# Two transformer blocks on one core: the first feed-forward chunk as wide pairs, banks in two sets, row factors spread through DRAM

## The chip, the cores and the metric

One NeuronCore of a Trainium2 chip. The metric is the device time of one execution in microseconds, lower is better. All data are float32 in and out.

## The reference, cut to what matters

A first block (retention and differential attention), then a second block of two layers. 256 tokens, width 1024. The change touches the four feed-forward networks (FFNs) of the second block and the projections for keys and values (kv) and queries (q):

```python
def rms_norm_2(x, g):
    xf = x.astype(jnp.float32)
    y = xf * lax.rsqrt(jnp.mean(xf * xf, axis=-1, keepdims=True) + RMS_EPS)
    return (y * g.astype(jnp.float32)).astype(x.dtype)

def swiglu_ffn(x, w_gate, w_up, w_down):            # D = 1024, F = 2816
    return (jax.nn.silu(x @ w_gate) * (x @ w_up)) @ w_down
...
    for layer in range(DEPTH_2):                    # 2 layers
        h = h + HALF_STEP * swiglu_ffn(rms_norm_2(h, ffn1_norm[layer]), ...)
        u = rms_norm_2(h, mix_norm[layer])
        ...                                         # layer 0: convolution; layer 1: stick-breaking attention,
                                                    # q from u, k and v from one projection after layer 0
        h = h + HALF_STEP * swiglu_ffn(rms_norm_2(h, ffn2_norm[layer]), ...)
```

## The kernel before, in words

The program is written out by hand per engine, with semaphores; nothing schedules it. Each engine's instructions stand in the order of its code. The stages of the second block are ffn1a, pw1, pw2 (convolution), ffn2a, kv, ffn1b, q, stick attention, o, ffn2b.

**Weights** come in slabs of 4 x 128 rows by 512 columns. SP loads slab k into one of four slots of `raw`; ACT rounds it (`cast`, L1174, `whi`), DVE takes the rest (`low`, L1550, `wlo`), so that a product in full precision is made of three products: high by high, low by high, high by low. The activations stand turned in `aT`, high and low halves side by side (`aT_hi`, `aT_lo`, 256 tokens each). A slot of `whi` is free when PE has done with the slab that held it (`half_done`, two counts a slab).

**FFN up side.** 2816 hidden columns are 11 chunks of 256 gate and 256 up columns, each chunk two slabs (half 0 and half 1 of the 1024 rows). Weights are the stationary operand, so hidden units come out on partitions. There are two forms. `turned_slab` (L639): per tile and row block three matmuls of 256 columns (L654, L656, L658) into one half bank, 48 a slab. `wide_slab` (L663): per tile and row block a pair, `wlo` by `aT_hi` in 256 columns (L678) and `whi` by both halves of `aT` in 512 (L680), 16 pairs a slab; the left half of a bank then holds the main sum and the right half a low sum, which must be added: ACT copies it out (`low_products`, L1351), DVE adds (`summed`, L1855, L1860). Chunk 0 of each FFN is turned, chunks 1 to 10 are wide. Chunks take pairs of banks in a ring of three pairs (`ffn_pair`: two of `acc`, one `att`), two pairs a chunk. PSUM's fourth pair is `tp`, for transposes. The order of slabs is (0, half 0), (1, half 0), (0, half 1), (1, half 1), then plain.

The rms norm's gain goes into `aT`, but its row factor `rs` does not: it depends on statistics that come late. It is applied to gate sums, where tokens lie along the free axis, so the 256 factors must lie in a row in each partition (`rsb`). DVE makes two diagonals from `rs` (`diagonal`, L1822), PE multiplies them with a matrix of ones (`spread_rs`, L692, in fp32), DVE copies the result (`rs_rows`, L1828). That is done in ffn1a, ffn2a, kv, q and ffn2b; ffn1b uses the factors of kv, and has dummy products in that place (L746). The up sum needs no factor: `rs_down`, half of it, is applied with the down product.

**Leaving a stage.** The second half of `h` is summed only after the last down slab, so four of eight blocks of `aT` are made inside the next stage: PE turns them into `tp` (`exit_fills`, L701) behind the first slab, ACT writes the high part (L1187), DVE the low part (L1565), and PE waits for `tp_lo` before the third slab. POOL makes `rs` from the statistics (L481 and L485, `residual_rs`). In ffn2b bank pair `att` holds part of the attention's output until the sum of the stage before.

```python
            order = [(0, 0), (1, 0), (0, 1), (1, 1)]          # pair_order
            ring = [acc_pair[(g + 1) % 2], att_pair, acc_pair[g % 2]]
            return ring[(2 * (c - 1) + up) % 3]               # ffn_pair
```

## Time and profile before

| | us |
|---|---|
| median of 3 runs (1265.23 to 1265.76) | 1265.34 |
| profiled execution | 1266.64 |
| its span, first to last instruction | 1264.9 |
| PE busy | 1255.5 (99%) |
| DVE busy | 827.1 (65%) |
| ACT busy | 619.9 (49%) |
| POOL busy | 85.1 (7%) |
| HBM read | 223 MB, 177 GB/s |
| mean granted clock of PE | 0.999 |

How to read it: a matmul's duration in the timeline runs from its start to its modelled end, and the next one starts before that, so what matmuls cost is read from starts. PE's share says that it is the engine to look at; what the others do shows only where PE waits for them.

### The profile page before, as it was taken

How to read it: one execution, taken by the hardware profiler on the slowest of the kernel's cores; microseconds unless marked ns; L12 is line 12 of the kernel's file. 1: busy time of each engine (PE TensorE's matmuls, PEld its weight loads, DVE VectorE, ACT ScalarE, POOL GpSimd, SP SyncE). 2: the span in 40 equal slices, each digit the busy share in tenths (PEclk: the TensorE clock that was granted, in tenths of full speed). 3: DMA queues.
4: the chain of work that ended last, by engine and by line, in shares of the span. 5: the costliest groups of instructions: out<-in, count | busy, mean ns of one | idle time of the engine just before them, and what ended most of it. 6: DMA issues, size and time to landing. Idle time of an engine off the chain costs nothing.

```text
span 1264.9 us, 16671 instructions
## 1 busy us (share of the span) xinstructions
PE 1255.5 (99%) x6814; PEld 1074.5 (85%) x6814; DVE 827.1 (65%) x953; ACT 619.9 (49%) x765; POOL 85.1 (7%) x122
## 2 busy tenths in 40 slices
PE   9999999999999999999999999999999999999998
PEld 7888877888988888879888889898888988988886
DVE  6565577667667656676777655656765666876653
ACT  5354566543555534444555543445553454555542
POOL 2223010101000002001000000000000110100000
PEclk9999999999999999999999999999999999999999
DMA  9654544456655566534565655656655513666640
GB/s 311 208 158 162 198 136 141 164 195 199 195 188 183 176 224 219 185 125 151 190 192 183 200 168 190 200 167 199 200 168 199 170 64 111 210 196 200 200 166 34
DMA packets 165388, 225.28 MB, mean 178 GB/s; under 512 B 7520, under 2 KB 106436, under 8 KB 165312
## 3 DMA queue, kind: packets, MB, share of 16 engines
q1 hardware_dynamic: 163488, 220.23, 53.3%
q0 software_dynamic: 1808, 3.98, 1.1%
q8 instruction: 54, 0.88, 0.3%
q14 instruction: 22, 0.18, 0.0%
q10 hardware_dynamic: 16, 0.00, 0.0%
HBM read 223.14 MB, written 1.05 MB: 177 GB/s over the span
## 4 chain that ended last, share of the span: by engine, by line
PE 97%; DVE 2%; ACT 1%; DMA 0%; issue 0%; SPq 0%; ACTq 0%
PE acc L680 15%; PE acc L621 15%; PE acc L623 15%; PE acc L622 15%; PE att L680 8%; PE acc L678 8%; PE att L678 4%; PE acc L654 2%; PE acc L658 2%; PE acc L656 2%; PE tp L701 1%; PE att L621 1%; PE att L623 1%; PE att L622 1%; DVE wlo L1550 1%; ACT whi L1174 0%
## 5 line engine op out<-in xcount | busy, mean ns | idle before, releaser
L1550 DVE TENSOR_TENSOR wlo<-raw,whi 128x2048 fp32r<-128x2048 f32 x205 | 467.7, 2289 | 165.4 <-ACT whi L1174 165.4
L1174 ACT ACTIVATE whi<-raw 128x2048 fp32r<-128x2048 f32 x205 | 388.6, 1912 | 92.8 <-PE acc L623 80.1
L680 PE MATMUL acc<-aT,whi 128*128 128x512 f32 x832 | 290.9, 391 | 0.0
L678 PE MATMUL acc<-aT,wlo 128*128 128x256 f32 x832 | 233.6, 281 | 0.0
L680 PEld LDWEIGHTS acc<-aT,whi 128*128 128x128 f32 x832 | 155.6, 187 | 33.8
L621 PE MATMUL acc<-whi,aT 128*128 128x512 f32 x432 | 172.9, 400 | 0.5 <-DVE wlo L1638 0.5
L623 PE MATMUL acc<-wlo,aT 128*128 128x512 f32 x432 | 168.9, 391 | 0.0
L622 PE MATMUL acc<-whi,aT 128*128 128x512 f32 x432 | 168.7, 391 | 0.0
L680 PE MATMUL att<-aT,whi 128*128 128x512 f32 x448 | 157.8, 391 | 0.0
L678 PEld LDWEIGHTS acc<-aT,wlo 128*128 128x128 f32 x832 | 157.3, 189 | 0.0
L621 PE MATMUL acc<-whi,hT_hi 128*128 128x512 f32 x348 | 135.7, 390 | 0.0
L622 PE MATMUL acc<-whi,hT_lo 128*128 128x512 f32 x348 | 135.5, 389 | 0.0
L623 PE MATMUL acc<-wlo,hT_hi 128*128 128x512 f32 x348 | 135.4, 389 | 0.0
L678 PE MATMUL att<-aT,wlo 128*128 128x256 f32 x448 | 125.4, 280 | 0.0
L680 PEld LDWEIGHTS att<-aT,whi 128*128 128x128 f32 x448 | 83.8, 187 | 18.4
L621 PEld LDWEIGHTS acc<-whi,aT 128*128 128x128 f32 x432 | 81.4, 188 | 18.2 <-issue 1.4
L623 PEld LDWEIGHTS acc<-wlo,aT 128*128 128x128 f32 x432 | 81.4, 188 | 17.6
L622 PEld LDWEIGHTS acc<-whi,aT 128*128 128x128 f32 x432 | 81.5, 189 | 15.9
L1351 ACT ACTIVATE low_part<-acc 128x512 f32<-128x512 f32 x52 | 31.0, 596 | 124.4 <-PE acc L680 124.4
L678 PEld LDWEIGHTS att<-aT,wlo 128*128 128x128 f32 x448 | 84.7, 189 | 0.0
L623 PEld LDWEIGHTS acc<-wlo,hT_hi 128*128 128x128 f32 x348 | 65.3, 188 | 13.6
L622 PEld LDWEIGHTS acc<-whi,hT_lo 128*128 128x128 f32 x348 | 65.3, 188 | 13.4
(332 smaller groups left out, 1588.1 us busy)
## 6 DMA issues: line engine op xcount, KB each, us to landing
raw<-in_ffn_w_gate_dram SPq DMA_DIRECT2D x88, 512.0 KB, 4.0
raw<-in_ffn_w_up_dram SPq DMA_DIRECT2D x88, 512.0 KB, 5.1
raw<-in_ffn_w_down_dram SPq DMA_DIRECT2D x88, 512.0 KB, 4.8
raw<-in_w_in_dram SPq DMA_DIRECT2D x70, 512.0 KB, 4.8
raw<-in_conv_w_pw_dram SPq DMA_DIRECT2D x24, 512.0 KB, 4.9
raw<-in_w_kv_dram SPq DMA_DIRECT2D x16, 512.0 KB, 5.0
raw<-in_ret_w_o_dram SPq DMA_DIRECT2D x8, 512.0 KB, 4.3
raw<-in_diff_w_o_dram SPq DMA_DIRECT2D x8, 512.0 KB, 4.2
```

Of the source, the lines that this page charges most:

```text
L621: mm_(banks[t][:, :], tokens(Th, kt, t), hi_, start=first_ and j == 0, stop=False)
L622: mm_(banks[t][:, :], tokens(Tl, kt, t), hi_, start=False, stop=False)
L623: last = mm_(banks[t][:, :], tokens(Th, kt, t), lo_, start=False, stop=last_ and j == len(kts) - 1)
L654: mm_(dst, whi[:, slot, cols], aT_hi[:, kt, :], start=half == 0 and j == 0 and n == 0, stop=False, skip_group_check=True)
L656: mm_(dst, whi[:, slot, cols], aT_lo[:, kt, :], start=False, stop=False, skip_group_check=True)
L658: last = mm_(dst, wlo[:, slot, cols], aT_hi[:, kt, :], start=False, stop=half == 1 and j == SLAB_K - 1, skip_group_check=True)
L678: mm_(bank[:, 0:T], wlo[:, slot, cols], aT_hi[:, kt, :], start=half == 0 and j == 0, stop=False, skip_group_check=True)
L680: last = mm_(bank[:, :], whi[:, slot, cols], aT[:, kt, :, :].rearrange("p a n -> p (a n)"), start=False, stop=half == 1 and j == SLAB_K - ...
L701: last = nc.tensor.transpose(tp[b % 2][:, q * T + t * P:q * T + (t + 1) * P], src(kt, t), ident[:, :])
L1174: A_(whi[:, slot, :], raw[:, slot, :], ACT.Copy).then_inc(hi_ready, 1)
L1351: A_(low_part[:, up, :, :], ffn_pair(name, c, up)[:, :, T:CW], ACT.Copy)\
L1550: V.tensor_tensor(wlo[:, slot, :], raw[:, slot, :], whi[:, slot, :].bitcast(F32), ALU.subtract)\
```

## The change

Chunk 0 of each FFN is made of wide pairs too. The chunks alternate between two sets of two pairs: even chunks take one `acc` pair and `att`, odd ones the other `acc` pair and `tp` (in ffn2b chunk 0 takes both `acc` pairs, chunk 1 `att` and `tp`). Since chunk 1's up part now lies in `tp`, where the fills of `aT` are still being read, PE's order is: chunk 0 half 0; the fills; chunk 1 half 0 gate part only; chunk 0 half 1; chunk 1 half 0 up part; chunk 1 half 1. The row factors are no longer spread by PE: POOL writes `rs` to a row in DRAM with two DMAs, waits, and reads it back into all partitions with one. The diagonals, the products and the copies go.

```diff
@@ build
         def ffn_pair(name, c, up):
 
             g = PLACE[name].g
-            ring = [acc_pair[(g + 1) % 2], att_pair, acc_pair[g % 2]]
-            return ring[(2 * (c - 1) + up) % 3]
+            first, second = acc_pair[g % 2], acc_pair[(g + 1) % 2]
+            if name == "ffn2b" and c < 2:
+                return [[first, second], [att_pair, tp_pair]][c][up]
+            return [[first, att_pair], [second, tp_pair]][c % 2][up]
 
 
         GAIN_STEP = 8
...
@@ build, engine POOL
                 pool.wait_ge(stat_ready, use + 1)
                 rsqrt(rs[:, use, :], rs_tmp[:, use, :], rs_tmp[:, use, :], 1.0, EPS, rs_ready)
                 pool.wait_ge(rs_ready, use + 1)
+                if use in SPREAD_USES:
+                    n = SPREAD_USES.index(use)
+                    for t in range(TT):
+                        pool.dma_start(rs_row[n, t * P:(t + 1) * P].rearrange("(p a) -> p a", a=1),
+                                       rs[:, use, t:t + 1]).then_inc(rs_written, 16)
                 nc.gpsimd.tensor_scalar(rs_down[:, use, :], rs[:, use, :], 0.5, None, ALU.mult)\
                     .then_inc(rs_down_ready, 1)
+                if use in SPREAD_USES:
+                    pool.wait_ge(rs_written, 32 * (n + 1))
+                    pool.dma_start(rsb[:, :], rs_row[n:n + 1, :].to_broadcast([P, T])).then_inc(rsb_ready, 16)
 
             residual_rs(RS_X)
             pool.wait_ge(rs_ready, 1)
...
@@ build, engine PE
                     if n == 1:
                         last.then_inc(half_done, 1)
 
-            def wide_slab(k, name, c, half):
+            def wide_slab(k, name, c, half, sides=(0, 1)):
 
                 w = PLACE[name]
                 pe.wait_ge(lo_ready, k + 1)
                 slot = k % SLOTS
-                for up in range(2):
+                for up in sides:
                     if half == 0 and c >= 2:
-
-                        pe.wait_ge(acc_free, 2 * (w.g + c - 1) + (up - 1) + 1)
+                        other = name == "ffn2b" and (c, up) == (2, 1)
+                        pe.wait_ge(acc_free, 2 * (w.g + c - 2) + up + 1 + other)
                     for n in range(FW // P):
                         bank = ffn_pair(name, c, up)[:, n, :]
                         f = up * (FW // P) + n
...
                                        stop=half == 1 and j == SLAB_K - 1, skip_group_check=True)
                     last.then_inc(half_done, 1)
 
-            def spread_rs(name, bank):
-
-                n = SPREADS.index(name)
-                pe.wait_ge(rdiag_ready, n + 1)
-                if n == 0:
-                    pe.wait_ge(pool_ready, 3)
-                for t in range(TT):
-                    last = mm_(bank[:, t * P:(t + 1) * P], ones[:, :], rdiag[:, t, :], start=True, stop=True)
-                last.then_inc(rsb_mm, 1)
-
             def fill(b, src, kts):
 
                 if b >= 2:
...
 
             def ffn_pe(name):
                 w = PLACE[name]
+                pe.wait_ge(tp_lo, w.b - 2)
+                pe.wait_ge(acc_free, 2 * (w.g - 1))
+                wide_slab(w.k, name, 0, 0)
                 if name == "ffn1b":
-                    pe.wait_ge(rsb_ready, SPREADS.index("kv") + 1)
-                for s, (c, half) in enumerate(pair_order(FC)):
-                    if s == 1 and name == "ffn1b":
-                        pe.wait_ge(acc_free, 2 * (w.g - 1) + 2)
-                        pe.wait_ge(rows_kept, 4)
-                        mm_(tp[0][:, 0:P], ones[:, :], ones[:, :], start=True, stop=True)
-                    elif s == 1:
-                        exit_fills(w.b - 2, w.g - 1, 1)
-                    pe.wait_ge(tp_lo, w.b - 2 if s < 2 else w.b)
-                    if c == 0:
-                        turned_slab(w.k + s, w.g, half)
-                    else:
-                        wide_slab(w.k + s, name, c, half)
-                    if s == 2 and name in SPREADS:
-                        spread_rs(name, tp[0])
-                    elif s == 2:
-                        for _ in range(TT):
-                            mm_(tp[0][:, 0:P], ones[:, :], ones[:, :], start=True, stop=True)
+                    pe.wait_ge(acc_free, 2 * (w.g - 1) + 2)
+                    pe.wait_ge(rows_kept, 4)
+                    pe.wait_ge(pool_ready, 3)
+                    mm_(tp[0][:, 0:P], ones[:, :], ones[:, :], start=True, stop=True)
+                else:
+                    exit_fills(w.b - 2, w.g - 1, 1)
+                wide_slab(w.k + 1, name, 1, 0, (0,))
+                pe.wait_ge(tp_lo, w.b)
+                wide_slab(w.k + 2, name, 0, 1)
+                wide_slab(w.k + 1, name, 1, 0, (1,))
+                wide_slab(w.k + 3, name, 1, 1)
+                for c in range(2, FC):
+                    for half in range(2):
+                        wide_slab(w.k + 2 * c + half, name, c, half)
                 ready = FC * FFN_AT[name]
                 for s in range(DOWN_SLABS):
                     k = w.k + 2 * FC + s
...
-                            pe.wait_ge(acc_free, 2 * (g - 1) + 1)
+                            pe.wait_ge(acc_free, 2 * (g - 2) + 1)
...
-                        if name in SPREADS:
-                            pe.wait_ge(rsb_ready, SPREADS.index(name) + 1)
                         exit_fills(w.b, w.g + FC, 0)
 
...
@@ build, engine ACT
 
                 def low_products(c):
                     for up in range(2):
-                        done(w.k + 2 * c + 1, up)
+                        if c:
+                            done(w.k + 2 * c + 1, up)
+                        else:
+                            act.wait_ge(half_done, 2 * w.k + 4 + up)
                         act.wait_ge(acc_free, 2 * (w.g + c))
                         A_(low_part[:, up, :, :], ffn_pair(name, c, up)[:, :, T:CW], ACT.Copy)\
                             .then_inc(low_copied, 1)
...
                     exit_hi(w.b - 2, 1, gain_in)
                 cast(w.k + 1 + AHEAD)
                 cast(w.k + 2 + AHEAD)
+                low_products(0)
                 silu(0)
-                cast(w.k + 3 + AHEAD)
+                cast(w.k + 3 + AHEAD, late=2)
                 for s in range(4, 2 * FC):
                     if s % 2 == 0:
                         low_products(s // 2 - 1)
...
@@ build, engine DVE
                                                       ALU.mult, ALU.mult)
                     last.then_inc(od_ready, 1)
 
-            def diagonal(use):
-
-                dve.wait_ge(rs_ready, use + 1)
-                for t in range(TT):
-                    last = V.tensor_scalar(rdiag[:, t, :], ident[:, :], rs[:, use, t:t + 1], None, ALU.mult)
-                last.then_inc(rdiag_ready, 1)
-
-            def rs_rows(name, bank):
-                n = SPREADS.index(name) + 1
-                dve.wait_ge(rsb_mm, n)
-                V.tensor_copy(rsb[:, :], bank[:, 0:T]).then_inc(rsb_ready, 1)
-                dve.wait_ge(rsb_ready, n)
+            def rs_rows(name):
+
+                dve.wait_ge(rsb_ready, 16 * (SPREADS.index(name) + 1))
 
             def turned_out(dst, g, ready, scale):
 
...
                     k = w.k + 2 * c + 1 if c else w.k + 2
                     gate, up = act_out[:, c % 2, :, :], hid[:, c % 2, :, :]
                     dve.wait_ge(lo_ready, k + AHEAD + 1)
-                    if c:
-                        dve.wait_ge(low_copied, copied + 2 * c - 1)
-                        V.tensor_tensor(gate, ffn_pair(name, c, 0)[:, :, 0:T], low_part[:, 0, :, :], ALU.add)\
-                            .then_inc(acc_free, 1)
-                        dve.wait_ge(acc_free, 2 * (w.g + c) + 1)
-                        V.tensor_tensor(gate, gate, spread, ALU.mult).then_inc(gate_ready, 1)
-                        dve.wait_ge(low_copied, copied + 2 * c)
-                        V.tensor_tensor(up, ffn_pair(name, c, 1)[:, :, 0:T], low_part[:, 1, :, :], ALU.add)\
-                            .then_inc(acc_free, 1)
-                    else:
-                        done(k, 1)
-                        one = [acc[w.g % 2][bank].rearrange("p (f n) -> p f n", n=T) for bank in range(2)]
-                        V.tensor_tensor(gate, one[0], spread, ALU.mult).then_inc(gate_ready, 1)
-                        dve.wait_ge(gate_ready, before + 1)
-                        V.tensor_copy(up, one[1]).then_inc(acc_free, 2)
+                    dve.wait_ge(low_copied, copied + 2 * c + 1)
+                    V.tensor_tensor(gate, ffn_pair(name, c, 0)[:, :, 0:T], low_part[:, 0, :, :], ALU.add)\
+                        .then_inc(acc_free, 1)
+                    dve.wait_ge(acc_free, 2 * (w.g + c) + 1)
+                    V.tensor_tensor(gate, gate, spread, ALU.mult).then_inc(gate_ready, 1)
+                    dve.wait_ge(low_copied, copied + 2 * c + 2)
+                    V.tensor_tensor(up, ffn_pair(name, c, 1)[:, :, 0:T], low_part[:, 1, :, :], ALU.add)\
+                        .then_inc(acc_free, 1)
 
                 def multiplied(c):
                     dve.wait_ge(silu_made, before + c + 1)
...
                 else:
                     exit_lo(w.b - 2, 1, gain_in)
                 low(w.k + 1 + AHEAD)
-                if name in SPREADS:
-                    diagonal(use)
                 low(w.k + 2 + AHEAD)
                 if name in SPREADS:
-                    rs_rows(name, tp[0])
+                    rs_rows(name)
                 summed(0)
                 low(w.k + 3 + AHEAD)
                 multiplied(0)
...
                     leave_ffn("ffn1b", RS_MIXB)
                 if s == 1:
                     exit_lo(pq.b - 2, 1, "mixb")
-                if s == 2:
-                    diagonal(RS_MIXB)
                 if s == 3:
-                    rs_rows("q", att[0])
+                    rs_rows("q")
 
                     turned_out(qT[:, 0:4, :], pq.g, lambda bank: dve.wait_ge(half_done, 2 * pq.k + 4 + bank),
                                SDK ** -0.5)
```

How it moves instructions, at three places.

PE in ffn2b, at the wait for `aT` (`tp_lo`) before chunk 0's second half. Before:

```order
L680 MATMUL att<-aT,whi 128x512
L678 MATMUL att<-aT,wlo 128x256
L680 MATMUL att<-aT,whi 128x512
L654 MATMUL acc<-aT,whi 128x256 [waits lo_ready,tp_lo]
L656 MATMUL acc<-aT,whi 128x256
```

After:

```order
L691 MATMUL att<-aT,whi 128x512
L689 MATMUL att<-aT,wlo 128x256
L691 MATMUL att<-aT,whi 128x512
L689 MATMUL acc<-aT,wlo 128x256 [waits lo_ready,tp_lo]
L691 MATMUL acc<-aT,whi 128x512
```

Before, `att` is chunk 1's up part, and 16 pairs stand between the fills and this wait; after, it is the gate part, and 8 do.

ACT in ffn2b, behind the casts of the slabs that chunks 0 and 1 need. Before:

```order
L1174 ACTIVATE whi<-raw 128x2048 [waits half_done,slab_landed3]
L1356 ACT_TABLE_LOAD
L1356 ACTIVATE act_out<-act_out 128x512 [waits gate_scaled]
L1174 ACTIVATE whi<-raw 128x2048 [waits half_done,slab_landed0]
L1351 ACTIVATE low_part<-acc 128x512 [waits acc_free,half_done]
L1351 ACTIVATE low_part<-att 128x512 [waits acc_free,half_done]
```

After:

```order
L1169 ACTIVATE whi<-raw 128x2048 [waits half_done,slab_landed3]
L1349 ACTIVATE low_part<-acc 128x512 [waits acc_free,half_done] x2
L1354 ACT_TABLE_LOAD
L1354 ACTIVATE act_out<-act_out 128x512 [waits gate_scaled]
L1169 ACTIVATE whi<-raw 128x2048 [waits half_done,slab_landed0]
L1349 ACTIVATE low_part<-att 128x512 [waits acc_free,half_done]
L1349 ACTIVATE low_part<-tp 128x512 [waits acc_free,half_done]
```

Two copies of chunk 0 stand ahead of the first silu; the next cast stands behind the silu in both.

POOL at the start of q. Before:

```order
L481 TENSOR_SCALAR rs_tmp<-rs_tmp 128x2 [waits stat_ready]
L485 TENSOR_TENSOR rs<-rs_tmp,mhalf 128x2 [waits pool_step]
L492 TENSOR_SCALAR rs_down<-rs 128x2 [waits rs_ready]
L581 MEMSET ntri 128x128 [waits half_done]
L582 AFFINE_SELECT ntri<-ntri 128x128 [waits pool_step]
```

After:

```order
L484 TENSOR_SCALAR rs_tmp<-rs_tmp 128x2 [waits stat_ready]
L488 TENSOR_TENSOR rs<-rs_tmp,mhalf 128x2 [waits pool_step]
L498 DMA rms_rows<-rs 128x1 [waits rs_ready]
L498 DMA rms_rows<-rs 128x1
L500 TENSOR_SCALAR rs_down<-rs 128x2
L504 DMA rsb<-rms_rows 128x256 [waits rms_row_written]
L592 MEMSET ntri 128x128 [waits half_done]
L593 AFFINE_SELECT ntri<-ntri 128x128 [waits pool_step]
```

Two DMAs, a wait for both to land and a third DMA stand between `rs` and the masks of the stick attention.

## Rows read from the trace of the kernel before

**Rows 1.** The page's busy shares, then the line of its chain by engine.
```profile
PE 1255.5 (99%) x6814; PEld 1074.5 (85%) x6814; DVE 827.1 (65%) x953; ACT 619.9 (49%) x765; POOL 85.1 (7%) x122
...
PE 97%; DVE 2%; ACT 1%; DMA 0%; issue 0%; SPq 0%; ACTq 0%
```

**Rows 2.** Waits of PE over the whole span: us in total, times, longest; first and last of five.
```profile
PE att L785 <- POOL ident L471: 1.6, 1, 1.6
...
PE att L621 <- DVE aT L2001: 0.2, 1, 0.2
```

**Rows 3.** Timeline of PE, ffn1a: start us, us, engine, line, operation.
```profile
310.77 0.28 PE L654 MATMUL acc<-aT,whi 128*128 128x256 f32 x1
...
316.52 1.03 PE L701 MATMUL tp<-ident,h 128*128 128x128 f32 x8
317.31 0.36 PE L678 MATMUL acc<-aT,wlo 128*128 128x256 f32 x1
```

**Rows 4.** Timeline of PE, ffn1a, from the spreading products to the down products.
```profile
328.69 0.61 PE L692 MATMUL tp<-rdiag,ones 128*128 128x128 f32 x4
329.05 0.36 PE L678 MATMUL acc<-aT,wlo 128*128 128x256 f32 x1
...
434.53 0.40 PE L621 MATMUL acc<-whi,hT_hi 128*128 128x512 f32 x1
```

**Rows 5.** Groups of PE by form: count | busy us, mean ns | idle before.
```profile
L746 PE MATMUL tp<-ones 128*128 128x128 f32 x4 | 0.6, 274 | 0.0
```

**Rows 6.** Timeline of DVE, ffn1a.
```profile
318.03 1.66 DVE L1565 SCALAR_TENSOR_TENSOR aT<-tp,gain,aT 128x256 fp32r<-128x256 f32 x4 [1.72 <-ACT aT L1187]
...
329.33 0.42 DVE L1828 COPY rsb<-tp 128x256 f32<-128x256 f32 x1 [3.88 <-PE tp L692]
```

**Rows 7.** Timeline, start of ffn2b: DVE, PE, ACT and DVE.
```profile
1083.14 1.65 DVE L1565 SCALAR_TENSOR_TENSOR aT<-tp,gain,aT 128x256 fp32r<-128x256 f32 x4
...
1074.95 0.28 PE L654 MATMUL acc<-aT,whi 128*128 128x256 f32 x1
...
1094.70 0.63 ACT L1356 ACTIVATE act_out<-act_out 128x512 f32<-128x512 f32 x1 [6.88 <-DVE act_out L1865]
...
1099.98 0.68 DVE L1855 TENSOR_TENSOR act_out<-acc,low_part 128x512 f32<-128x512 f32 x1
```

**Rows 8.** Timeline of POOL: a DMA issue, and rs of ffn2b.
```profile
32.10 0.57 POOL L504 DMA_DIRECT2D v_r<-in_diff_lq_dram  x1
...
1083.35 0.70 POOL L485 TENSOR_TENSOR rs<-rs_tmp,mhalf 128x2 f32<-128x2 f32 x1
```

**Rows 9.** DMA issues of POOL and one of SP: KB each, median us from issue to landing.
```profile
h<-in_x_dram POOLq DMA_DIRECT2D x2, 512.0 KB, 4.3
...
out_dram<-h SPq DMA_DIRECT2D x2, 512.0 KB, 2.8
...
g_out<-in_final_norm_dram POOLq DMA_DIRECT2D x1, 512.0 KB, 6.6
...
v_r<-in_diff_lk_dram POOLq DMA_DIRECT2D x2, 32.0 KB, 7.0
...
dqk_g<-in_diff_q_norm_g_dram POOLq DMA_DIRECT2D x2, 0.2 KB, 4.3
```

**Rows 10.** Timeline of PE and POOL, stage q.
```profile
1016.63 0.70 PE L1090 MATMUL att<-qT,kT 64*128 64x256 f32 x4
...
1002.70 0.70 POOL L485 TENSOR_TENSOR rs<-rs_tmp,mhalf 128x2 f32<-128x2 f32 x1
```

**Rows 11.** Timeline of PE and POOL, start of ffn2a.
```profile
583.42 0.28 PE L654 MATMUL acc<-aT,whi 128*128 128x256 f32 x1
...
588.16 2.62 POOL L485 TENSOR_TENSOR rs<-rs_tmp,mhalf 128x2 f32<-128x2 f32 x1
```

**Rows 12.** Instructions of line 481: ns min/median/max; and DVE's timeline beside issues.
```profile
L481 POOL TENSOR_SCALAR rs_tmp<-rs_tmp x7: 183/2164/2171, 24.1 to 1081.1; 128x2 f32<-128x2 f32 x7
...
30.34 2.29 DVE L1550 TENSOR_TENSOR wlo<-raw,whi 128x2048 fp32r<-128x2048 f32 x1
```

More of the change, by code:

```diff
@@ L218, in build @@
         ones = sb("ones", [P, P], to=second)
-        rdiag = sb("rdiag", [P, TT, P], to=second)
         rsb = sb("rsb", [P, T], to=second)
@@ L1068, in _ @@
                     slab(pkv.k + s, pkv.g + c, half, aT_hi, aT_lo)
-                if s == 2:
-                    spread_rs("kv", att[0])
             ffn_pe("ffn1b")
@@ L1078, in _ @@
             turned_slab(pq.k + 2, pq.g, 1)
-            spread_rs("q", att[0])
             turned_slab(pq.k + 1, pq.g + 1, 0, range(2, 4))
@@ L2061, in _ @@
                     kept_lo(pkv.b, 0, "ffn1b")
-                if s == 2:
-                    diagonal(RS_KV)
                 if s == 3:
-                    rs_rows("kv", att[0])
+                    rs_rows("kv")
                 if s in (3, 4):
```

7 lines of the change are left out of this document (4 added, 3 removed).

## The prediction

> **What bounds the kernel now.** I read the page's busy shares and its chain first, then PE's waits, then the timeline at the places that the change touches. PE is busy for 1255.5 of 1264.9 us, and 97% of the chain that ended last is PE [rows 1]. PE's list of waits has five entries, from 1.6 us down to 0.2, none in an FFN, in kv or in q [rows 2]. So time is won or lost in two ways only: fewer or cheaper PE instructions, and new waits of PE. DVE (65%) and ACT (49%) matter only where PE would wait for them. The clock granted to PE is 9 tenths or more in all slices of the page and 0.999 in the mean, its level of 2.4 GHz, with PE busy throughout.
>
> The profiled execution took 1266.64 us, 1.30 above the median of the three timed runs (1265.34). I make the sum against the profiled one and take the same off the median. A measurement of this kernel can tell about 0.2%, 2.5 us, from no change.
>
> **Cheaper products of chunk 0.** A turned slab is 48 matmuls of 256 columns. The first of ffn1a runs from 310.77 to the transposes at 316.52: 5.75 us [rows 3]. A wide slab is 16 pairs. From 329.05 to the first down product at 434.53 stand 19 slabs, 304 pairs, in 105.48 us: 0.347 us a pair, 5.55 a slab [rows 4]. Each of four FFNs has two turned slabs: 8 x 0.20 = **1.6 us** less of PE, all on the path.
>
> **Spreading products gone.** The diagonal matmuls of ffn1a take PE from 328.69 to 329.05, and the first matmul behind them lasts 0.36 us where one behind other such products lasts 0.28: 0.44 us [rows 3, 4]. By the code there are five such places (ffn1a, ffn2a, kv, q, ffn2b), and the dummies of L746 in ffn1b are four matmuls of the same form [rows 5]. 6 x 0.44 = **2.6 us**, all on the path. PE has 4.2 us less in all.
>
> **What is added beside PE, at nothing.** Per FFN: two ACT copies of low products (0.6 us each, as the page's L1351) and one DVE operation of 0.7 more; DVE loses two diagonals and a copy. In ffn1a DVE stood idle for 3.88 us before its copy of the row factors [rows 6], and ACT waited for DVE meanwhile. If that cover went, the delay would lie in the path costed below. Chunks from 2 up now wait for the chunk two before instead of the one before, so their slack grows. The factors, though, come by a slower way.
>
> **The split of chunk 1.** PE waits for the last two fills of aT before chunk 0's second half. Before, 16 pairs covered the copies; now 8 do (2.78 us, and 0.08 for the change from transposes). In ffn1a DVE begins them at 318.03 and needs 1.66, so ends 3.17 after the transposes began; these take 0.79, so PE now comes 0.79 + 2.86 = 3.65 after their start: 0.4 in hand [rows 3, 6]. In ffn2b DVE does a low part first and ends the copies at 1083.14 + 1.65 = 1084.79. There PE starts at 1074.95, and comes at 1074.95 + 5.55 + 0.79 + 2.86 = 1084.15 [rows 7]. **A new wait of 0.7 us**, with 0.06 for the semaphore. Everything behind it in PE's queue moves by as much.
>
> **The factors through DRAM.** This cost is in no row, and it decides the result. POOL writes rs in two DMAs of 4-byte pieces, waits for both, and issues a DMA that lands 128 copies of one 1 KB row. From the end of rs it takes 0.1 us to the first issue, 0.57 to the second [rows 8], then a landing, 0.1, then a landing. Call the sum c. The nearest row for the write is dqk_g, 4-byte pieces over partitions, 4.3 us: I take 4.5. For the read there are 4.3 (x again) and 6.6 (g_out, a broadcast), of 512 KB each [rows 9]; I take 5.1, the lower half, as it has a quarter of their bytes. **c = 10.3 us**. Bounds: 2.8 twice (the output's stores, another queue, nothing beside them) gives 6.4; 7.0 twice (v_r) gives 14.8.
>
> Where does PE feel c? In **ffn2b** chunk 2's up part goes into att, which chunk 1's gate must have left. When the factors land, DVE adds and scales gate 0 (two operations of 0.7, 1.4); then silu, the cast, the low part, the multiply and the add of gate 1 follow, in the rows of before from 1094.70 to 1099.98 + 0.68: 5.96 [rows 7]. With latencies 7.45 us. PE gets there, behind the wait above, at 1084.85 + 5.55 + 2.78 + 5.55 + 2.78 = 1101.51. So the factors must land by 1094.06. Rs is ready at 1083.35 + 0.70 = 1084.05 [rows 8]. Limit: c = 10.0. With 10.3, **0.3 us of wait**. In **q**, PE reaches the first stick score at 1016.63 - 0.44 = 1016.2 and needs both qT scalings (1.3 us) done. Rs ends at 1002.70 + 0.70 = 1003.40: limit c = 11.4 [rows 10]; no wait. Kv needs the factors a slab of 5.75 later than q, so c = 17 would do there. In the ring of ffn2a the rs ends 590.78 - 583.42 = 7.4 us into the stage, and the wait is for chunk 0 or for the low part of slab 5, at most 7.45 us behind the factors; PE comes 5 x 5.55 + 0.87 = 28.6 us into the stage, so c = 13.7 is free [rows 11]; ffn1a has an earlier rs. POOL now blocks until the write has landed. Behind it stand the masks of the stick attention and the final gain, with 5 us and more to spare.
>
> **Sum.** 4.2 - 0.7 - 0.3 = 3.2 us less: 1266.64 goes to 1263.4, the median 1265.34 to **1262.1**.
>
> One thing could stretch c. POOL's arithmetic is held while DVE runs L1550: L481 has a median of 2.16 us beside it and a minimum of 0.18. Its DMA issues aren't: L504 takes 0.57 at 32.10, beside the L1550 from 30.34 to 32.63 [rows 8, 12]. The Trainium skill, "SBUF — State Buffer", section "Who interferes with whom", says that a DVE operation with two SBUF inputs contends with GpSimd's reads, and infers that descriptor writing needs the write side. The trace agrees. The same page's box on DVE blocking DMA says that descriptor writing starves under the two-port modes; stretched to L1550 that rule would be the rival "held issues" below.
>
> **Rivals.**
> *Short way* (chance 0.25). c is under 10 and the 0.3 goes: 1265.34 - 4.2 + 0.7 = 1261.8. For it: the output's stores landed in 2.8 us. Against: 0.2 KB took 4.3 on this queue [rows 9]. The Trainium skill, "DMA: Bandwidth & Descriptors", section "Anatomy of one DMA — SWDGE (gpsimd) path", gives some 2 us plus the bytes for one such DMA: an estimate of c near 5 by that page, which is this case. No row here is as short.
> *Forecast* (0.35): c from 10 to 11, 1261.8 to 1262.8.
> *Longer way* (0.20). Above 11.4 q pays too: the waits are 0.7 + (c - 10.0) + (c - 11.4). c = 12 gives 1264.4, c = 13 gives 1266.4.
> *Held issues* (0.07). The second write of ffn2b, issued at 1084.7, is held by an L1550 for 2.3 us, q's read by some 1.4: waits of 2.6 and 0.3 beside the 0.7, 1264.7. Against it stands the 0.57 above.
> *Slower* (0.13): the round trip becomes the bound. From c = 13.7 the waits (0.7 + 3.7 + 2.3 = 6.7) pass the 4.2 by 0.2%; at 14.8 they are 0.7 + 4.8 + 3.4, with 1.1 in ffn2a's ring: 1271.1. For it: v_r landed in 7.0 us, and a write of 4-byte pieces to DRAM is in no row. Against: v_r stood in a filled queue, these don't.
> That the change doesn't do what it says gets no chance: which instructions go is plain from the order.
>
> **The numbers.** Faster by over 0.2% means under 1262.8: short way and forecast, 0.60. Within: longer way and held issues, 0.27. Slower: 0.13. The range goes from 1261.0 (no wait at all gives 1261.1) to 1267.0, which leaves out the slower case and little else.
>
> **What would show it.** PE: no threes of 256-column matmuls in the FFNs, no diagonals, pairs at 0.347 in chunk 0 too. A wait of PE for aT in ffn2b of 0.7, none in ffn1a. From the end of rs to the landing of rsb 10.3 us, in five places. A wait of PE at chunk 2's up part in ffn2b of 0.3, none before the stick scores. I am wrong if c is above 11.4, if PE waits in ffn1a, ffn2a or kv, or if the pairs of chunk 0 are slower.

## The result, and the profile after

The changed kernel takes 1291.09 us (median of 4 runs, 1288.58 to 1294.64), the kernel before 1265.43 (4 runs, 1265.23 to 1265.76): ratio 1.0202, 95% interval 1.0190 to 1.0214. It is **2.0% slower**; the forecast was 1262.1, with 1261.0 to 1267.0 as its range. The profiled execution took 1290.27 us, with a span of 1288.5 and a mean granted clock of 0.991.

The page's busy shares and the chain by engine, against [rows 1]:

```profile
PE 1261.3 (98%) x6662; PEld 1071.5 (83%) x6662; DVE 825.1 (64%) x942; ACT 624.1 (48%) x773; POOL 97.3 (8%) x137
...
PE 88%; DMA 5%; DVE 3%; POOL 1%; ACT 1%; issue 1%; SPq 0%; ACTq 0%; DVEq 0%
```

PE has 152 instructions fewer and is busy for 5.8 us *more*, and DMA now holds 5% of the chain, where it had none. The waits of PE, against [rows 2] (engine, line waited for: us in total, times, longest):

```profile
PE acc L689 <- DVE act_out L1844: 8.7, 3, 4.3
PE att L1085 <- DVE qT L1825: 6.9, 1, 6.9
PE att L783 <- POOL ident L474: 1.6, 1, 1.6
PE acc L632 <- issue: 1.4, 1, 1.4
PE att L689 <- DVE act_out L1844: 1.2, 1, 1.2
...
PE acc L689 <- DVE aT L1564: 0.4, 1, 0.4
```

All but the third are new, 18.6 us in sum. And what DVE waited for in front of them:

```profile
DVE act_out L1844 <- DMA rsb<-rms_rows: 34.5, 3, 13.5
DVE qT L1825 <- DMA rsb<-rms_rows: 9.6, 1, 9.6
DVE kT L1825 <- DMA rsb<-rms_rows: 8.2, 1, 8.2
```

So the row factors come late in all five places. Timeline of POOL and DVE in ffn2b, against [rows 7, 8]:

```profile
1098.65 0.72 POOL L488 TENSOR_TENSOR rs<-rs_tmp,mhalf 128x2 f32<-128x2 f32 x1
1099.66 1.18 POOL L498 DMA_DIRECT2D rms_rows<-rs  x2 [0.30 <-POOL rs L488]
1100.87 3.70 POOL L500 TENSOR_SCALAR rs_down<-rs 128x2 f32<-128x2 f32 x1
1110.98 0.59 POOL L504 DMA_DIRECT2D rsb<-rms_rows  x1 [6.42 <-DMA rms_rows<-rs]
1118.00 0.69 DVE L1844 TENSOR_TENSOR act_out<-acc,low_part 128x512 f32<-128x512 f32 x1 [13.51 <-DMA rsb<-rms_rows]
```

Rs ends at 1099.37, the writes are issued from 1099.66, the read only 11.3 us later, and DVE starts on the factors at 1118.00: c, the way from the end of rs to the landed factors, is 18.6 us. Counted alike, c is 17.9 in ffn1a, 17.7 in ffn2a, 18.6 in kv, 18.4 in q; the forecast had 10.3. The page's two entries for the new DMAs (KB each, median us to landing), against [rows 9]:

```profile
rsb<-rms_rows POOLq DMA_DIRECT2D x5, 128.0 KB, 7.0
...
rms_rows<-rs POOLq DMA_DIRECT2D x10, 0.5 KB, 9.4
```

The second cost is what the waits do to PE's clock. Windows of the trace (us; busy time and count of PE, PEld, DVE, ACT, POOL; granted clock; DMA share; GB/s) behind the four longest waits, in ffn1a, ffn2a, q and ffn2b:

```profile
334.00:340.00 6.00, 4.74 (x18) 4.15 (x19) 3.65 (x4) 3.40 (x4) 0.00 (x0) 0.72 0.13 44
612.00:617.00 5.00, 5.00 (x22) 4.30 (x21) 3.10 (x4) 3.40 (x4) 0.00 (x0) 0.66 0.00 0
1028.00:1034.00 6.00, 4.68 (x26) 3.94 (x27) 3.41 (x5) 1.96 (x3) 0.00 (x0) 0.50 0.06 19
1119.00:1124.00 5.00, 5.00 (x16) 4.11 (x16) 3.10 (x3) 3.40 (x4) 0.00 (x0) 0.50 0.02 6
```

A granted 0.50 is the level of 1.2 GHz. Behind each of these waits PE's products run at that level for 3.4 to 5 us: a pair starts every 0.64 us, not every 0.347. The waits before them were 1.8, 2.5, 6.9 and 4.3 us. In kv, where PE is held for 1.4 us, the clock doesn't fall.

Stage by stage, by the same operation in both timelines: ffn1a +2.9 us, ffn2a +3.5, kv +1.1, ffn1b -0.8, q to the first stick score +6.5, from there to the first cumulative product +2.7 (8.0 us for 5.3), ffn2b with the stick stage's rest +8.6. That is 24.5. The profiled execution was 0.6 ahead of that of before when ffn1a began (the transposes of ffn1a's entry start at 303.78 and were at 304.41), so it is 23.9 behind at ffn2b's down products; the spans differ by 23.6.

### The profile page after: what moved, and what is told of

Read it like the earlier page. It is cut to its first block, busy times and chain, and to the rows that moved or that the text cites. A ratio compares the mean times of both kernels' runs of the same rounds, so it can differ in the third digit from the quotient of the medians.

```text
span 1288.5 us, 16337 instructions
## 1 busy us (share of the span) xinstructions
PE 1261.3 (98%) x6662; PEld 1071.5 (83%) x6662; DVE 825.1 (64%) x942; ACT 624.1 (48%) x773; POOL 97.3 (8%) x137
## 4 chain that ended last, share of the span: by engine, by line
PE 88%; DMA 5%; DVE 3%; POOL 1%; ACT 1%; issue 1%; SPq 0%; ACTq 0%; DVEq 0%
PE acc L632 14%; PE acc L634 14%; PE acc L633 14%; PE acc L691 11%; PE att L691 6%; PE acc L689 6%; PE tp L691 5%; PE att L689 3%; DMA rms_rows<-rs 3%; PE tp L689 3%; DMA rsb<-rms_rows 2%; PE tp L702 1%; DVE wlo L1549 1%; PE acc L665 1%; PE acc L667 1%
## 5 line engine op out<-in xcount | busy, mean ns | idle before, releaser
L1549 DVE TENSOR_TENSOR wlo<-raw,whi 128x2048 fp32r<-128x2048 f32 x205 | 467.2, 2289 | 166.2 <-ACT whi L1169 166.1
L691 PE MATMUL acc<-aT,whi 128*128 128x512 f32 x704 | 253.4, 398 | 0.0
L689 PE MATMUL acc<-aT,wlo 128*128 128x256 f32 x704 | 200.4, 285 | 9.1 <-DVE act_out L1844 8.7
L691 PEld LDWEIGHTS acc<-aT,whi 128*128 128x128 f32 x704 | 134.5, 191 | 29.8
L689 PEld LDWEIGHTS acc<-aT,wlo 128*128 128x128 f32 x704 | 135.6, 193 | 10.4 <-issue 9.5
L691 PE MATMUL att<-aT,whi 128*128 128x512 f32 x384 | 135.4, 392 | 0.0
L691 PE MATMUL tp<-aT,whi 128*128 128x512 f32 x320 | 112.8, 391 | 0.0
L689 PE MATMUL att<-aT,wlo 128*128 128x256 f32 x384 | 107.7, 281 | 1.2 <-DVE act_out L1844 1.2
L689 PE MATMUL tp<-aT,wlo 128*128 128x256 f32 x320 | 89.6, 280 | 0.0
L691 PEld LDWEIGHTS att<-aT,whi 128*128 128x128 f32 x384 | 71.8, 187 | 15.9
L1349 ACT ACTIVATE low_part<-acc 128x512 f32<-128x512 f32 x44 | 26.2, 595 | 113.2 <-PE acc L691 113.2
```

Source lines behind the costliest of these rows:

```text
L689: mm_(bank[:, 0:T], wlo[:, slot, cols], aT_hi[:, kt, :], start=half == 0 and j == 0, stop=False, skip_group_check=True)
L691: last = mm_(bank[:, :], whi[:, slot, cols], aT[:, kt, :, :].rearrange("p a n -> p (a n)"), start=False, stop=half == 1 and j == SLAB_K - ...
L1349: A_(low_part[:, up, :, :], ffn_pair(name, c, up)[:, :, T:CW], ACT.Copy)\
L1549: V.tensor_tensor(wlo[:, slot, :], raw[:, slot, :], whi[:, slot, :].bitcast(F32), ALU.subtract)\
```

## Experiments

**1 and 2. Each half of the change alone.** The first kernel keeps the wide pairs, the two sets of banks and the split of chunk 1, and has TensorE spread the factors as before. The second is the kernel before with the factors sent through DRAM.

```diff
 # wide_pe_spread, on the changed kernel
-                        pool.dma_start(rs_row[n, t * P:(t + 1) * P].rearrange("(p a) -> p a", a=1),
-                                       rs[:, use, t:t + 1]).then_inc(rs_written, 16)
...
-                    pool.dma_start(rsb[:, :], rs_row[n:n + 1, :].to_broadcast([P, T])).then_inc(rsb_ready, 16)
...
-                wide_slab(w.k + 2, name, 0, 1)
+                if name in SPREADS:
+                    wide_slab(w.k + 2, name, 0, 1, (0,))
+                    spread_rs(name, tp[0])
+                    wide_slab(w.k + 2, name, 0, 1, (1,))
```

> The change with PE's own spreading put back (diagonal products into tp between the two sides of chunk 0's second half), wide pairs and bank sets kept. Theory A (the slow way of the factors makes all of the loss, the wide pairs are a gain): 8 x 0.20 and 0.44 for the dummies less, some 0.5 for the wait for aT in ffn2b, so 1263.9 (1263 to 1265.5), no wait of PE at chunk 2 and a granted clock of 0.999. Theory B (the new banks or the split order lose too): 1268 or more, with waits of PE in the first slabs of the FFNs.

> The kernel before with only the spreading changed: the factors go through DRAM, chunk 0 stays turned, the ring of three pairs stays. Theory A: some 18 us from rs to the landed factors in five places; since in the old ring chunk 2's up part waits for chunk 1's gate in every FFN, the delays are larger than in the change: about 5.7, 6.5 and 9 us in ffn1a, ffn2a and ffn2b, 1.5 in kv, 7 in q with 2.7 behind it at the lower clock, less 2.2 of products: 1290 to 1297. Theory B: under 1280.

The wide pairs alone: **1264.38 us** (10 runs), ratio to before 0.9992 (0.9983 to 1.0001), and PE's only new entry in the list of waits is 0.4 us for aT in ffn2b. The median is 0.5 above the expected 1263.9 and inside its range; the interval takes in 1, so a gain isn't shown. The factors through DRAM alone: **1295.88** (4 runs), ratio 1.0247 (1.0227 to 1.0267), inside the expected 1290 to 1297, clock 0.991, with these waits:

```profile
PE acc L687 <- DVE hid L1849: 10.5, 3, 4.9
PE att L1082 <- DVE qT L1817: 5.8, 1, 5.8
PE acc L630 <- issue: 2.1, 1, 2.1
PE acc L687 <- DVE act_out L1837: 1.9, 3, 0.9
```

The whole loss belongs to the way through DRAM. It costs 30 us without the wide pairs and 27 with them (1291.09 - 1264.38).

**3. The clock.** Products of ones (28 calls, 56 matmuls in the trace) go to a bank that nobody reads yet, ahead of the wait in q.

```diff
+                    for _ in range(28):
+                        mm_(att[0][:, 0:P], ones[:, :], ones[:, :], start=True, stop=True)
```

> The change with 28 dummy products of ones (some 6 us, into a bank that the first score overwrites) ahead of the wait before the first stick score. They compute nothing that is used. Theory C (PE's idle time lowers the granted clock, and the work behind it pays): the wait shrinks to 1 us, the first score starts at the same time, but the clock stays at 1.00 behind it and the stretch from the first score to the first cumulated product takes 5.3 us as before instead of 8.0: 2.7 us less than the change. Theory D (the products behind the wait are slow for another reason, such as late data): no gain.

It took 1289.67 us (4 runs, 1288.40 to 1293.14), 1.4 below the changed kernel. PE's timeline, first score and first cumulative product, and the windows from there:

```profile
1033.25 0.70 PE L1087 MATMUL att<-qT,kT 64*128 64x256 f32 x4 [1.16 <-DVE qT L1827]
...
1038.55 0.67 PE L1097 MATMUL att<-sp,ntri 128*128 128x256 f32 x2
```

```profile
1034.00:1040.00 6.00, 6.00 (x53) 5.52 (x50) 4.51 (x5) 4.42 (x6) 1.04 (x3) 1.00 0.01 3
```

The scores now take 0.70 us a group, as before [rows 10], not 1.23; the clock is 1.00, and from score to cumulative product there are 5.3 us, as before, not 8.0. So the clock's 2.7 us in q are shown at the place. The medians differ by 1.4 us only, less than the runs of either kernel scatter, and don't show it: the way of the factors was 18.9 us in this execution, and ffn2a, which the edit doesn't touch, lost 5.9 us in it against 3.5 in the changed kernel's. The waits vary that much from run to run.

**4 to 7. What is slow in the round trip.** Each kernel changes the write: where it goes, its pieces, their distance, the queue. The first three, and the two of experiment 9, compute without the rms factors (the broadcast reads a row of an input, or the identity's row was written), so they serve for their times alone. Where it goes:

```diff
 # row_in_sbuf: the same pieces of 4 bytes into one row of SBUF
-                        pool.dma_start(rs_row[n, t * P:(t + 1) * P].rearrange("(p a) -> p a", a=1),
+                        pool.dma_start(rs_row[0:1, t * P:(t + 1) * P],
                                        rs[:, use, t:t + 1]).then_inc(rs_written, 16)
-                    pool.dma_start(rsb[:, :], rs_row[n:n + 1, :].to_broadcast([P, T])).then_inc(rsb_ready, 16)
+                    pool.dma_start(rsb[:, :], A["norm_g"][0:1, 0:T].to_broadcast([P, T])).then_inc(rsb_ready, 16)
```

> The change with the two DMAs of 4-byte pieces writing to a row in SBUF instead of DRAM; the read then takes a row of an input instead, so the factors are left out. Theory E (small writes to DRAM are what is slow, and hold up the DMA engines): from the first issue to the read's issue 5 us instead of 10.3 to 11.3, and weight loads issued meanwhile land in 5 us instead of 9.5 to 14. Theory F (any DMA of 4-byte pieces, or POOL's queue itself): as in the change.

1265.59 us in one run. From the first write's issue to the read's issue: 5.5, 6.6, 5.1, 5.0 and 6.5 us in the five places, where the changed kernel has 10.3, 11.1, 11.3, 10.6 and 11.3. Next, the pieces' form, and their distance in DRAM:

```diff
 # row_pieces_whole: two whole pieces of 512 bytes in DRAM
-                        pool.dma_start(rs_row[n, t * P:(t + 1) * P].rearrange("(p a) -> p a", a=1),
-                                       rs[:, use, t:t + 1]).then_inc(rs_written, 16)
+                        pool.dma_start(rs_row[n:n + 1, t * P:(t + 1) * P],
+                                       ident[0:1, :]).then_inc(rs_written, 16)
 # pieces_apart: pieces of 4 bytes in DRAM, each in a row of 512 bytes of its own
+        rs_far = nc.dram_tensor("rms_far", (2 * len(SPREADS) * P, P), F32, kind="Internal").ap()
+                        pool.dma_start(rs_far[(2 * n + t) * P:(2 * n + t + 1) * P, 0:1],
...
+                    pool.dma_start(rsb[:, :], A["norm_g"][0:1, 0:T].to_broadcast([P, T])).then_inc(rsb_ready, 16)
```

> The change with each of the two writes replaced by one contiguous row of 512 bytes (the first row of the identity) into the same DRAM row, and the same read of it by 128 partitions. The factors are left out of the wide copies by this (the identity's row stands in their place). In the changed kernel's profile, from the first write's issue to the read's issue 10.3 to 11.3 us go by. Theory E1 (the pieces of 4 bytes in DRAM are the cost): here 4.5 to 6.5 us, the whole way from the factors to the first scaled copy about 11 to 12 us, the weight loads issued meanwhile land in about 5 us, the whole 1263 to 1267 us. Theory E2 (any write to DRAM that a read of the same row follows is slow, whatever its form): still 9 to 11 us, and the whole at 1284 to 1292 us.

> The change with its pieces of 4 bytes written to DRAM places 512 bytes apart, and the broadcast reading a row of the norm's factors in its place (so the rms factors are left out of the wide copies). If the cost of the write comes from neighbouring pieces falling in the same stretch of DRAM, the time from the first write's issue to the read's issue falls from 10.3 to 11.3 us to about 5 to 7 us, and the whole to 1263 to 1270 us. If each piece in DRAM has its price wherever it lies, it stays at 9 to 11.5 us and the whole at 1283 to 1292 us.

1264.14 and 1263.56 us, one run each. In row_pieces_whole the read is issued 4.6 to 6.2 us after the first write and reads the row that was just written, so a read behind a write isn't slow by itself. But its source differs too (512 bytes of one partition, not a column over 128), and pieces_apart is the closer comparison. The view of the write's line (who waited for it; us to landing, min/median/max), changed kernel first:

```profile
  POOL rsb L504: 44.0, 5
...
DMA to landing us min/median/max: 5.7/9.4/10.4
```

```profile
  POOL rsb L504: 16.2, 5
...
DMA to landing us min/median/max: 3.9/4.2/5.2
```

The second is pieces_apart: 256 pieces of 4 bytes in DRAM for each use, as in the changed kernel, and they land in 4.2 us. The read is issued 4.8 to 6.1 us after the first write. So neither DRAM nor the pieces' size is slow; 128 pieces **side by side** in 512 bytes are. In this kernel c is 10.4 in ffn1a, 12.9 in ffn2a and 11.8 in ffn2b. And the queue that issues:

```diff
 # writes_by_act, for each of the five uses, behind ACT's exit of the fill
+                act.wait_ge(rs_ready, use + 1)
+                for t in range(TT):
+                    act.dma_start(rs_row[n, t * P:(t + 1) * P].rearrange("(p a) -> p a", a=1),
+                                  rs[:, use, t:t + 1]).then_inc(rs_written, 16)
```

> The change with its two writes of 4-byte pieces issued from ACT's queue instead of POOL's, each stage's behind the exit whose scaling uses the factors on ACT; the read stays on POOL. If the cost lies in the pieces at the DRAM, the write still takes 9 to 11 us from its issue until the read can be issued, weight loads still land late, and the whole is 1287 to 1297 us (ACT's issues, some of them later than POOL's, can only add). If the cost lies in POOL's queue (its descriptors are written by POOL's software), the write lands in 4 to 5 us, the weight loads keep their 5 us, and the whole is 1264 to 1272 us.

1292.20 us in one run, as expected of a cost at the DRAM. The write's landing is 8.7 us instead of 9.4, from its first issue to the read's 9.5 to 12.2 us go by (9 to 11 were expected), and PE's new waits come to 18.7 us instead of 18.6: POOL's queue isn't the cause.

**8. The dose.**

```diff
+                        pool.dma_start(rs_again[n, t * P:(t + 1) * P].rearrange("(p a) -> p a", a=1),
+                                       rs[:, use, t:t + 1]).then_inc(rs_written, 16)
...
-                    pool.wait_ge(rs_written, 32 * (n + 1))
+                    pool.wait_ge(rs_written, 64 * (n + 1))
```

> The change with every write of factors issued twice (the second time into another row), and the read waiting for all four. If the pieces are served one after the other at a price each, the time from the first write's issue to the read's issue goes from 10.3 to 11.3 us to 17 to 21 us, and the whole to 1325 to 1350 us, with the waits of TensorE for scaled copies 7 to 10 us longer in each of the five stages. If the time is mostly a fixed latency, it rises only by the two further issues of 0.58 us, to about 12 us, and the whole to 1294 to 1300 us.

1318.27 us in one run. From the first write to the read's issue 15.7, 17.5 (ffn1a, ffn2a), 16.5 (kv), 15.2 (q) and 15.4 us (ffn2b), where there were 10.3 to 11.3; c is 21.8 to 24.5. With 256 pieces apart it is 5 to 6 us, with 256 side by side about 11, with 512 about 16: some 5 us for each 256 pieces, an estimate of 20 ns a piece, after 5 to 6 us for the trip. (The two further issues, 1.1 us in all, are in the last step, so it may be somewhat less.) The expectation of a price for each piece was too high by this: the way is a little under its 17 to 21 in four of five places, the whole 7 us under its 1325 to 1350, and PE's waits grow by 3.4 to 6.9 us, not 7 to 10. But both lie far above those of a fixed latency, about 12 us and 1294 to 1300.

**9. How near is side by side.** pieces_apart with rows of 16, then of 4 elements in DRAM (64 and 16 bytes between the starts of pieces).

> pieces_apart with the 4-byte pieces 64 bytes apart in DRAM in place of 512 (the rms factors are left out of the wide copies, as there). With 512 bytes between them the read could be issued 4.8 to 5.9 us after the first write's issue, with none between them 10.3 to 11.3 us. If only pieces that share 64 bytes or fewer hold each other up, it is 4.8 to 6 us again and the whole 1263 to 1266 us. If the stretch in which they do so is 512 bytes, it is 9 to 11.3 us and the whole 1283 to 1292 us. In between, a time between them.

> pieces_apart with the 4-byte pieces 16 bytes apart (the rms factors are left out of the wide copies, as there). At 64 bytes apart the read was issued 4.6 to 6.1 us after the first write's issue, side by side 10.3 to 11.3 us. If pieces that share a stretch of 64 bytes hold each other up one by one, four share it here in place of sixteen: 5 to 8 us if the price goes with the number that share one, 9 to 11.3 us if it goes with every piece that isn't alone, and 4.6 to 6.1 us if the stretch is 16 bytes or less.

First write to read's issue at 64 bytes 4.7, 6.1, 5.0, 4.6 and 5.8 us, whole 1264.22; at 16 bytes 5.1, 7.1, 4.9, 4.8 and 6.4 us, whole 1265.12 (one run each). Nearly all of the price is gone at 16 bytes already (one place, ffn2a, is 1.1 above the 64-byte run), so four pieces in 64 bytes hardly pay it; between 4 and 16 nothing was tried. The Trainium skill, "Collectives: The Full Stack", section "Rules for kernel authors", asks for collectives' buffers aligned to 32 bytes, which keeps the hardware from a read-modify-write. No run here shows one, and two pieces that share 32 bytes (the 16-byte run) didn't pay the price; which mechanism holds the pieces up isn't shown.

**10. A version without that cost.** The row lies in SBUF, and 128 partitions read it from there; nothing of the computation is left out. Two variants follow: one with aT's low half ahead of a weight slab's in ffn2b (also on wide_pe_spread), one with POOL's halved factors behind the read.

```diff
 # through_sbuf, on row_in_sbuf
+                    pool.dma_start(rsb[:, :], rs_row[0:1, :].rearrange("p (o n) -> p o n", o=1).to_broadcast([1, P, T])).then_inc(rsb_ready, 16)
 # through_sbuf_at and pe_spread_at
+                if name == "ffn2b":
+                    exit_lo(w.b - 2, 1, gain_in)
                 low(w.k + 0 + AHEAD)
...
-                else:
+                elif name != "ffn2b":
                     exit_lo(w.b - 2, 1, gain_in)
```

> The change with the row of factors kept in SBUF in place of DRAM: the pieces of 4 bytes are written into one SBUF row, and 128 partitions read that row; nothing is left out. Earlier runs showed that the write into such a row (row_in_sbuf) and writes to DRAM 512 bytes apart (pieces_apart) let the read be issued 4.8 to 6.6 us after the first write's issue, against 10.3 to 11.3 us in the changed kernel. If the cost is in neighbouring pieces in DRAM alone, the whole way from the factors to the first scaled copy is about 12 us here, TensorE's waits for scaled copies are 2 us in all at most, and the whole is 1263.5 to 1266 us, a gain of 0 to 2 us on the kernel before. If 128 reads of one SBUF row are slow (no run has shown them so far), the read lands later than the 5.3 to 7.0 us seen from DRAM, and the whole is 1268 us or more.

> through_sbuf, and in ffn2b VectorE writes the low half of aT ahead of a weight slab's low half instead of behind it. TensorE's wait of 0.4 us for aT there should go, and the whole be 0.3 to 0.5 us below through_sbuf. Rival: the weight slab's low half is then late and TensorE waits for it by as much, and the two are the same within 0.1 us.

> wide_pe_spread (the wide pairs with the factors spread by TensorE) with the same swap in ffn2b. That kernel took 1264.38 us with a wait of 0.4 us for aT; without the wait about 1264.0 us, 0.3 to 0.5 us below it and 1.2 to 1.6 us below the kernel before. Rival: the wait moves to the weight slab and it stays at 1264.4 us.

> through_sbuf with POOL's halved factors computed behind the issue of the read in place of ahead of it (nothing left out). In ffn2b they took 3.7 us and the read was issued 6.2 us after the first write, against 4.8 to 5.3 us in kv and q. If they hold the read, it is now issued 4.5 to 5.5 us after the first write there, the way of the factors in ffn2b falls from 13.2 to 11.5 to 12.5 us, TensorE's wait there from 2.7 to 1 to 2 us, and the whole from 1267.0 to 1264.5 to 1266 us. If the write itself is what is late in ffn2b, nothing changes by more than 0.3 us.

| kernel (11 runs each) | us | ratio to before (95%) |
|---|---|---|
| through_sbuf | 1267.01 (1265.17 to 1268.68) | 1.0011 (1.0003 to 1.0020) |
| through_sbuf_at | 1263.52 (1263.35 to 1265.31) | 0.9986 (0.9977 to 0.9995) |
| pe_spread_at | 1265.31 (1264.82 to 1265.65) | 0.9997 (0.9988 to 1.0006) |
| sbuf_half_late | 1267.30 (1265.32 to 1268.85) | 1.0011 (1.0002 to 1.0020) |

through_sbuf gives back 24 of the 26 us, but it is still 1.5 us slower than before, by an interval clear of 1, and misses its own expectation by 1: c is 13.2 in ffn2b (11.6 to 13.0 elsewhere), and PE waits 2.7 us there. Three points:

- The halved factors (L500, 3.70 us in ffn2b) aren't the cause. Behind the read they leave its issue where it was, 6.4 us after the first write, and PE waits 3.0. The expected gain didn't come, and the rival stands: the write itself is late.
- The swap removes aT's wait, and PE waits for the weight slab instead, 1.7 us: `PE acc L680 <- DVE wlo L1561: 1.7, 1, 1.7` in pe_spread_at. There it gains nothing: 1265.31 is 0.9 above wide_pe_spread (on another chip, where before takes the same time), where the forecast had 0.3 to 0.5 less and the rival no difference. The rival had the mechanism, and the new wait is 1.3 us longer than the one that went.
- In through_sbuf_at the same swap gains 3.5 us, which neither theory had. Timelines of POOL in ffn2b, through_sbuf and then through_sbuf_at:

```profile
1077.09 2.16 POOL L484 TENSOR_SCALAR rs_tmp<-rs_tmp 128x2 f32<-128x2 f32 x1 [32.78 <-DVE rs_tmp L1595]
...
1080.34 1.18 POOL L498 DMA_DIRECT2D rs_row<-rs  x2 [0.29 <-POOL rs L488]
...
1086.55 0.59 POOL L504 DMA_DIRECT2D rsb<-rs_row  x1 [1.30 <-DMA rs_row<-rs]
```

```profile
1076.92 0.19 POOL L484 TENSOR_SCALAR rs_tmp<-rs_tmp 128x2 f32<-128x2 f32 x1 [32.79 <-DVE rs_tmp L1595]
...
1078.20 1.18 POOL L498 DMA_DIRECT2D rs_row<-rs  x2 [0.30 <-POOL rs L488]
...
1081.02 0.59 POOL L504 DMA_DIRECT2D rsb<-rs_row  x1 [1.37 <-DMA rs_row<-rs]
```

The factors come 5.7 us earlier, for two reasons. The first is seen in POOL's first row: its step for rs takes 2.16 us beside VectorE's L1549 in the one, and 0.19 in the other, where the swap has moved L1549 away, so rs is ready 2.1 us earlier. The second is the way: the read is issued 6.2 us after the first write in the one, 2.8 in the other. SP issues two weight loads of 512 KB at 1079.22 and 1079.64 in the first, just ahead of the writes. In the second they go out at 1081.80, since VectorE frees their buffer later. c falls to 9.7, and PE's 2.7 us are gone. This reads as small DMAs queued behind large ones, 3.4 us of it. In the other four stages of both kernels a weight load is issued in the 1.2 us ahead of the writes, and there 4.8 to 6.2 us go by, which agrees. But it rests on traces that differ in more than that, and wasn't isolated.

through_sbuf_at is the fastest of the versions that compute everything: 2.0 us below the kernel before on the same chip, an interval clear of 1, and 0.14%. It is 1.8 us below pe_spread_at, which has the same swap and PE's own spreading.

## Why the prediction was wrong

**What bounds the kernel, and where c is felt: right.** With c as measured, the forecast's own limits come close to PE's waits in three stages. In q, 18.4 - 11.4 = 7.0, measured 6.9. In ffn2b, 18.6 - 10.0 = 8.6: up to chunk 2's up part PE waited 4.3 for chunk 0's banks, which the forecast did not see as a place of its own, then ran slow products for 2.3 more, and waited 1.2 at the place that was named, 7.8 in all. At c = 11.8 in ffn2b (pieces_apart) the limit gives 1.8, measured 1.3. In kv, 18.6 against 17: 1.6, measured 1.4 (the list says "issue"). For ffn2a the limit of 13.7 was too strict: with 17.7 it would be 4.0, and PE waited 2.5 (in another execution, q_kept_busy's, 3.8 at c = 19.0). Ffn1a, for which no limit was worked out, has c = 17.9 and a wait of 1.8.

**The cheaper products: right.** pieces_apart has every such saving and no late factors up to q. Its stages lose 0.8 (ffn1a), 0.8 (ffn2a), 0.4 (kv), 0.8 (ffn1b) and 0.4 us (q): 3.2, where the forecast has 3 x 0.84 + 2 x 0.44 = 3.4. Pairs run at 0.347 in chunk 0. The rows that show it start and end ffn1a, in pieces_apart, where before had 304.41 and 434.53 [rows 4]: 129.33 us against 130.12.

```profile
303.05 1.03 PE L702 MATMUL tp<-ident,h 128*128 128x128 f32 x8
...
432.38 0.40 PE L632 MATMUL acc<-whi,hT_hi 128*128 128x512 f32 x1
```

**The wait for aT: right.** The list has 0.43 us; from start to start, as the forecast counted its 0.7, PE comes 0.59 later. There is none in ffn1a.

```profile
1100.14 0.39 PE L689 MATMUL acc<-aT,wlo 128*128 128x256 f32 x1 [0.43 <-DVE aT L1564]
```

**The factors through DRAM: the term that failed.** "I take 4.5" for the write: from its first issue to the read's 10.3 to 11.3 us went by, where the sum had 5.2. "I take 5.1" for the read: 7.0. The price was taken from dqk_g, whose 4-byte pieces are *read* from DRAM and land over partitions of SBUF [rows 9]; a write whose pieces are neighbours in DRAM had no row, as the forecast itself said under its slower rival. Its upper bound, 7.0 twice, was a landing of 32 KB, and c came out 3 to 4 us above it. So a bound from the nearest rows was no bound: the operation differed in direction and destination, and the range should have gone on above 14.8. The forecast's own signs of being wrong (c above 11.4, waits of PE in ffn1a, ffn2a and kv) all came. Part of the excess goes beyond the writes: weight loads issued around them land late too. The DMA view of 1097 to 1112 us, changed kernel:

```profile
raw<-in_ffn_w_gate_dram SPq DMA_DIRECT2D x3, 512.0 KB, 11.4
raw<-in_ffn_w_up_dram SPq DMA_DIRECT2D x3, 512.0 KB, 13.0
```

In the same window of before these are 4.1 and 5.1, and in pieces_apart 3.9 and 5.1. In the other stages of the changed kernel they are late too, by less (8.9 and 10.4 us in the window 312 to 330, against 4.0 and 5.0 before). In q the DMA engines are shown as busy from 1017 to 1020.5 us and move little:

```profile
1017.00:1020.50 3.50, 3.50 (x32) 3.50 (x31) 1.42 (x1) 0.00 (x0) 0.00 (x0) 1.00 1.25 28
```

DMA's share is 1.25 at 28 GB/s; before has 0.97 at 313 GB/s between 1011 and 1016 us. The Trainium skill, "DMA: Bandwidth & Descriptors", section "Anatomy of one DMA — SWDGE (gpsimd) path", with its 2 us plus the bytes gave c near 5; this case measures 18, and 9.7 in through_sbuf_at's ffn2b, where the pieces alone landed in 1.9 us.

**The clock: a term that was missing.** The forecast priced waits at their length. Four of them are also followed by products at 1.2 GHz (that the wait is the cause is shown by experiment in q, and read from the order of events in the others): six pairs of 0.64 in ffn1a and six in ffn2a (6 x 0.29 = 1.8 each), 2.7 in q, eight pairs in ffn2b (2.3), 8.6 us in all. Waits of 18.6, plus 8.6, less the 4.2 saved, make 23.0 of the 24.2 us to explain (23.6 between the spans, and the 0.6 of the start). Most of the rest lies in ffn2b: counted from start to start, its three waits cost 6.8 us, where the list has 5.9.

The slower rival had the mechanism, the places and its sign, at a chance of 0.13 and a price of 1271.1. c of 18 in place of 14.8 (8.6 us more of waits than its 10.0) and the clock (8.6) make most of the other 20 us.

## What to carry to other kernels

A column of SBUF that is written to DRAM as neighbouring 4-byte pieces costs, by this case's estimate, about 20 ns a piece, and loads issued around it landed late too; put such pieces 16 bytes or more apart, or, so that they can be read as one row, collect them in a row of SBUF (either lands in 4 to 5 us). When a price has no row, ask in which direction and to what memory the nearest row goes before calling it a bound. Where TensorE is the bound and a new wait lasts some 2 us or more, allow for slow products behind it: here they were 8.6 us behind 18.6 us of waits. They followed every wait of 3.8 us or more, and about half of those from 1.8 to 3.0.

## What the runs showed of the hardware

- 128 pieces of 4 bytes in 512 bytes of DRAM land in 9.4 us (5.7 to 10.4) from POOL's queue and in 8.7 from ACT's; 512 bytes apart in 4.2 (3.9 to 5.2), 16 bytes apart in 4.2 (3.9 to 6.2), in a row of SBUF in 4.6 (4.0 to 5.6).
- Loads of 512 KB issued around them land in 11.4 and 13.0 us (medians, ffn2b) instead of 4.1 and 5.1.
- After waits of PE of 1.8, 2.5, 4.3 and 6.9 us products ran at the lower level for 3.4 to 5 us (changed kernel). Over all traces every wait of 3.8 us or more in the stages concerned is followed by it, and none of 1.7 or less. Between them it fell either way: after 1.8, 2.0 (q_kept_busy), 2.5 (twice), 2.7 and 3.0 (dram_spread_alone) it came; after 1.9 (writes_by_act), 2.1 (dram_spread_alone, kv), 2.4 (pieces_64 and pieces_16) and 3.0 (sbuf_half_late) it didn't. Two windows in ffn2b, behind 2.7 us in through_sbuf and behind 3.0 in sbuf_half_late:

```profile
1098.00:1102.00 4.00, 1.33 (x5) 1.19 (x5) 3.96 (x6) 2.00 (x3) 0.00 (x0) 0.77 0.30 90
```

```profile
1098.00:1102.00 4.00, 1.45 (x8) 1.31 (x9) 3.96 (x6) 2.07 (x2) 0.00 (x0) 1.00 0.34 93
```
